# A fused two-layer PEER/MLA trunk: one placed list of stage parts, and each addition of v given to an engine by a model of both

## The reference, cut to what matters

```python
S, D, DEPTH = 512, 1024, 2            # tokens, width, layers
def peer_mixer(h, w_q, sub_keys, u, v):          # both layers
    q = (h @ w_q).reshape(B, S, 8, 2, 128)
    s = einsum('bshpc,hpnc->bshpn', q, sub_keys)
    top_s, top_i = top_k(s, 16)
    best_s, pos = top_k(top_s[..., 0, :, None] + top_s[..., 1, None, :], 16)
    idx, gate = indices at pos, softmax(best_s)            # 8 x 16 = 128 experts per token
    a = einsum('tkd,td->tk', u[idx], h)                    # u, v: 16384 x 1024
    return einsum('tk,tkd->td', gate * gelu(a), v[idx])

for i in range(2):
    h = rmsnorm(x, mix_norm[i])
    x = x + (pool_mixer(h) if i == 0 else mla_mixer(h, ...))    # mla: 8 heads, causal, after shared_kv(x)
    x = x + peer_mixer(rmsnorm(x, ffn_norm[i]), ...)
    g = sigmoid(rmsnorm(x, ple_norm[i]) @ ple_wg[i])
    x = x + g * (p[i] @ ple_wp[i])
return rmsnorm(x, final_norm)
```

## Time and profile before

| | |
|---|---|
| median of 3 runs | 2887.83 us (2886.12 to 2888.53) |
| the profiled execution | 2894.77 us, span 2893.0 us |
| busy share of the span | PE 79%, DVE 74%, POOL 44%, ACT 37% |
| moved from HBM | 1175 MB, 1074 MB of it by the gathers |
| mean rate over the span | 406 GB/s |
| mean granted TensorE clock | 0.905 |

### The profile page before, as it was taken

The page is one execution under the profiler, slowest core; times in us unless marked ns, Lnnn a source line. Parts: engine busy times, 40 slices in busy tenths (PEclk is TensorE's granted clock), DMA queues, the critical chain, the costliest instruction groups (busy, mean ns, idle before and its releaser), DMA issues.

```text
span 2893.0 us, 23323 instructions
## 1 busy us (share of the span) xinstructions
PE 2281.1 (79%) x6572; PEld 1176.2 (41%) x6572; DVE 2142.1 (74%) x4486; ACT 1072.7 (37%) x3181; POOL 1278.6 (44%) x1029
## 2 busy tenths in 40 slices
PE   6787777977879987888687999799967788766555
PEld 4444233522534543455253455346624333222112
DVE  6877768885797667757979766676696788677776
ACT  2433324333244433632324443364332244333222
POOL 2353543454443444444433344444344344555652
PEclk8999988998999998999899999899989899987777
DMA  8999999999999999999999999999999999999995
GB/s 357 416 386 419 413 420 397 409 420 420 420 383 411 420 420 420 419 420 420 395 420 394 418 410 419 420 400 398 420 392 420 419 387 415 419 420 420 420 420 234
DMA packets 164787, 1175.37 MB, mean 406 GB/s; under 512 B 18481, under 2 KB 19889, under 8 KB 23601
## 3 DMA queue, kind: packets, MB, share of 16 engines
q0 software_dynamic: 147456, 1073.81, 90.4%
q1 hardware_dynamic: 16624, 98.24, 8.3%
q10 hardware_dynamic: 576, 1.84, 0.2%
HBM read 1171.71 MB, written 2.10 MB: 406 GB/s over the span
## 4 chain that ended last, share of the span: by engine, by line
PE 35%; DMA 34%; DVE 19%; ACT 5%; issue 4%; POOL 2%; DVEq 0%; SPq 0%; ACTq 0%; POOLq 0%
DMA slot<-in_uv,idx 34%; PE acc L931 19%; DVE slot L1638 7%; DVE X L1629 2%; PE B L685 2%; PE M L603 2%; PE B L603 2%; PE M L873 2%; POOL slot L580 2%; PE M L685 1%; ACT diag L1156 1%; PE B L873 1%; ACT w L1150 1%; DVE SD L1266 1%; DVE top_u L1271 1%
## 5 line engine op out<-in xcount | busy, mean ns | idle before, releaser
L931 PE MATMUL acc<-slot,diag 128*128 128x512 f32 x2904 | 1558.1, 677 | 576.8 <-ACT diag L1156 575.3
L580 POOL DMA_INDIRECT slot<-in_uv,idx x1024 | 1278.3, 1248 | 1571.9 <-PE acc L931 1106.0
L1638 DVE CUSTOM_DVE_ANT_0 slot<-slot,HP 128x1024 f32<-128x1024 f32 x1024 | 1244.1, 1221 | 602.6 <-DMA slot<-in_uv,idx 593.1
L931 PEld LDWEIGHTS acc<-slot,diag 128*128 128x128 f32 x2904 | 575.0, 210 | 1416.9 <-ACT diag L1156 846.0
L1148 ACT ACTIVATE act_a<-a 128x1 f32<-128x1 f32 x1024 | 206.7, 202 | 1629.7 <-DVE a L1638 1628.6
L1629 DVE SCALAR_TENSOR_TENSOR X<-slot,w,X 128x1024 f32<-128x1024 f32 x297 | 380.6, 1282 | 24.0 <-ACT w L1150 23.9
L1150 ACT ACTIVATE w<-act_a,gate 128x1 f32<-128x1 f32 x1024 | 301.7, 295 | 33.2
L1156 ACT ACTIVATE diag<-cst,w 128x128 f32<-128x128 f32 x726 | 291.5, 402 | 23.8
L685 PE MATMUL B<-TT,w 128*128 128x256 f32 (+1 forms) x448 | 88.0, 351 | 0.0
L685 PE MATMUL M<-TT,w 128*128 128x256 f32 (+1 forms) x448 | 87.3, 349 | 0.0
L685 PEld LDWEIGHTS B<-TT,w 128*128 128x128 f32 x448 | 77.3, 193 | 20.6 <-issue 13.0
(11 more groups left out here) (201 smaller groups left out, 1559.9 us busy)
## 6 DMA issues: line engine op xcount, KB each, us to landing
w<-in_wq SPq DMA_DIRECT2D x28, 1024.0 KB, 9.1
slot<-in_uv,idx POOLq DMA_INDIRECT x1024, 14.3
w<-in_ple_wg SPq DMA_DIRECT2D x8, 1024.0 KB, 9.0
w<-in_w_o SPq DMA_DIRECT2D x8, 1024.0 KB, 9.2
w<-in_w_dq SPq DMA_DIRECT2D x6, 1024.0 KB, 9.5
w<-in_w_uq_nope SPq DMA_DIRECT2D x8, 768.0 KB, 8.5
w<-in_ple_wp SPq DMA_DIRECT2D x5, 1024.0 KB, 10.5
slot<-in_wq SPq DMA_DIRECT2D x4, 1024.0 KB, 15.6
```

The lines of the kernel that those rows point to most:

```text
L580: nc.gpsimd.indirect_dma_start(out=slot[s][:], out_offset=None, in_=uv[g // NC], in_offset=bass.IndirectOffsetOnAxis(ap=idx[:, g % HPB, k: ...
L931: last = nc.tensor.matmul(acc[:, half * 512:half * 512 + 512], diag[adds_on_pe(n) % DIAGS][:], slot[s][:, D + half * 512:D + half * 512 + ...
L1638: nc.vector.tensor_tensor_reduce(out=slot[s][:, 0:D], in0=slot[s][:, 0:D], in1=HP[:, g % HPB, :], scale=1.0, scalar=0.0, op0=ALU.mult, op1 ...
```

## The change

1. **One list.** `STEPS`, `BESIDE`, `PARTS`, `LATER` and the two lanes go. `PASSES[g]` is one list of (stage, part). `WORK` gives for each part its microseconds on VectorE and on PE; `weight` turns that into gathers, and `starts_of` lays the parts one after the other by their weights (those after `rank1` stretched by up to 1.4), up to gather 112. The rank stages stand in the list like the others: `asked_second` puts `rank1` behind `asks1`, and `woven` mixes the rank stages of the next chunk among the keys, queries or gates.
2. **Additions.** `adders` walks the pass with a clock for VectorE and one for PE, adds each part's work where it stands, and gives each addition of v to VectorE where PE is further behind by more than 0.3 us, else to PE. The counts per pass become 24, 23, 46, 51, 46, 55, 28 and 16 (289 in all, 298 before).
3. **Norms.** ScalarE squares all chunks of a stage first (with a `STEP` between) and takes one square root over them; before, one root for each chunk.
4. **Small steps.** More `STEP`s and part borders in `pool`, `fnorm` and `trig` on VectorE.

The pieces of weights, their order and the total of bytes are the same, as is the work except for the square roots.

```diff
-ADDS_ON_DVE = (32, 28, 32, 44, 32, 42, 26, 64)
+DVE_HEAD, DVE_TAIL = 3, 2
...
+WORK = {
+    "pool": lambda g, n: [(0, 0), (1, 0)] + [(2.6, 3.7), (2.3, 3.7)] * n + [(2.6, 0)],
...
+DVE_FREE, PE_FREE, DVE_ADD, PE_ADD, DOT = 1.4, 0.9, 1.3, 1.75, 1.3
+
+def weight(st, part):
+    dve, pe = WORK[st[0]](*st[1:])[part]
+    both = (dve / DVE_ADD + pe / PE_ADD) / (DVE_FREE / DVE_ADD + PE_FREE / PE_ADD)
+    return max(both, dve / DVE_FREE, pe / (PE_FREE + PE_ADD * DVE_FREE / DVE_ADD))
...
+def starts_of(g):
+    begin, last = (0 if g == 0 else DVE_HEAD - 1), KSEL - 16
+    weights = [weight(*p) for p in PASSES[g]]
+    soon = 1 + max([-1] + [i for i, (st, _) in enumerate(PASSES[g]) if st[:2] == ("rank1", g)])
+    rest = sum(weights[soon:])
+    scale = min(STRETCH, (last - begin - sum(weights[:soon])) / rest) if rest else 1
+    scaled = [w if i < soon else w * scale for i, w in enumerate(weights)]
+    return [int(begin + sum(scaled[:i])) for i in range(len(weights) + 1)]
...
+def adders():
...
+        unit = DOT + DVE_FREE
+        dve = pe = 0.0
+        for k in range(KSEL):
+            dve = max(dve, k * unit) + stage_work[k][0] + DOT
+            pe = max(pe, k * unit) + stage_work[k][1]
+            head = g > 0 and k < DVE_HEAD
+            tail = g == PAIRS - 1 and k >= KSEL - DVE_TAIL
+            behind_dve, behind_pe = dve - k * unit - DOT, pe - dve
+            on_dve = head or tail or behind_pe > behind_dve + 0.3
+            if on_dve:
+                dve += DVE_ADD
+            else:
+                pe = max(pe, dve + 1.1) + PE_ADD
+            found.append(on_dve)
...
-            def norm(stage, g0, src, width, i=0):
+            def norms(stage, g0, srcs, width, i=0):
...
+                for j, src in enumerate(srcs):
+                    if j:
+                        yield STEP
+                        act.wait_ge(squared, n + j)
+                    nc.scalar.activation(sq_out[:, 0:width], src, ACT.Square, accum_out=ss[:, n + j:n + j + 1]
+                                         ).then_inc(squared, 1)
+                act.wait_ge(squared, n + len(srcs))
+                nc.scalar.activation(rms[:, n:n + len(srcs)], ss[:, n:n + len(srcs)], ACT.Sqrt, bias=eps,
+                                     scale=1.0 / width).then_inc(normed, len(srcs))
```

More of the change, by code:

```diff
@@ L176, with top16s @@
         "add": [("ple_wp", [0])], "wp": [("ple_wp", [0])], "tail": [("ple_wg", [0, 1, 2, 3])]}
[L181 to L204, removed]
-}
+def top16s(n):
+    return 3.3 * n
@@ L344, in begin, with finish @@
+                spread.clear()
+    def finish():
+        while spread:
+            step()
+    def begin(st, part):
+        finish()
         stage, g0, n = st
@@ L961, in fnorm_stage @@
                 act.wait_ge(x_ready, before("x_ready", "fnorm", g0))
-                for i in range(n):
-                    norm("fnorm", g0, X[:, (g0 + i) % NC, :], D, i)
+                yield from norms("fnorm", g0, rows(g0, n), D)
                 yield
@@ L1004, in latent_stage @@
                 act.wait_ge(x_ready, before("x_ready", "latent", g0))
-                for i in range(n):
-                    norm("latent", g0, X[:, (g0 + i) % NC, :], D, i)
+                yield from norms("latent", g0, rows(g0, n), D)
                 for _ in range(4):
@@ L1009, in latent_stage @@
                 act.wait_ge(weights_used, used("w_dkv", g0, 0))
-                for i in range(n):
-                    norm("latent", g0, MB[i][:, 0:KVR], KVR, n + i)
+                yield from norms("latent", g0, [MB[i][:, 0:KVR] for i in range(n)], KVR, n)
             def keys_stage(g0, n):
@@ L1028, in dq_stage @@
                 act.wait_ge(weights_used, used("w_dq", g0, 2))
[L1029 to L1030 removed]
+                yield from norms("dq", g0, [MB[i][:, 0:QR] for i in range(n)], QR)
             def uq_stage(g0, n):
@@ L1085, in enorm_stage @@
                 act.wait_ge(x_ready, before("x_ready", "enorm", g0))
-                for i in range(n):
-                    norm("enorm", g0, X[:, (g0 + i) % NC, :], D, i)
+                yield from norms("enorm", g0, rows(g0, n), D)
                 yield
@@ L1100, in add_stage @@
                 if g0 >= NC:
-                    for i in range(n):
-                        act.wait_ge(x_ready, before("x_ready", "add", g0) + i + 1)
-                        norm("add", g0, X[:, (g0 + i) % NC, :], D, i)
+                    act.wait_ge(x_ready, before("x_ready", "add", g0) + n)
+                    yield from norms("add", g0, rows(g0, n), D)
                     yield
@@ L1112, in tail_stage @@
                 act.wait_ge(half_summed, 2)
-                norm("tail", g0, X[:, c, :], D)
+                yield from norms("tail", g0, rows(g0, 1), D)
                 act.wait_ge(hat_scaled, 1)
```

227 lines of the change are left out of this document (127 added, 100 removed).

## The result

The kernel with the change takes 2921.94 us (median of 4 runs, 2916.32 to 2923.66), before it is 2888.18 us in the same comparison: 1.0106 times as long, with an interval of 1.009 to 1.0121. That is 31 us **slower** (the two medians themselves stand 33.8 us apart), where I had forecast 25 us less and a range up to 2884 us. The profiled execution has a span of 2921.8 us. It is the slowest of its four, and the profile of the kernel before lies 6.6 us above its median, so a length read from one profile is good to some us only.

What follows compares the result with a forecast made beforehand. The prediction took the DMA roof of 420 GB/s as the bound. Its terms, -20.4 - 10.6 + 3.5 + 4 - 1.3 = -24.8 us from a median of 2887.8, gave 2863 us, forecast 2852 to 2870, range 2842 to 2884.

Steps and rivals of the forecast that it cites:

- The prediction's own sign of being wrong: Middle slices lose 45 us or more in new places, or the last pass runs under 420 GB/s with PE full.
- The bound: Whole kernel: DMA at 420 GB/s is the roof, 2798 us of the span's 2893; only the middle's 51.8 us is open.
- The rank stretches: Six stretches with rank stages lost 30.7 us; moving stages and additions leaves a third and takes back 20.4 us.
- PE's stages and the scattered losses: Pooling, attention of the last chunk and scattered places lost 10.0 + 11.2 us; half, 10.6 us, is recovered.
- The block of 25.8: Passes 2 and 4, gather 56: worst remaining VectorE block, 25.8 us of work, nearly fits 25 to 28 us of DMA.
- Norm and scaling: Ten places start norm and reciprocal at one gather; VectorE waits at least 4.1 us each; +4 us, 0 to 8.
- The fewer square roots: ScalarE saves 15 of 37 square roots of 0.29 us on an engine at 37%; effect nothing.
- The ring: Pass 0, third query of asks1: closer weight-buffer reuse makes PE stand about 5.4 us; +3.5 us overall, 0 to 7.
- The tail: End of the last pass: one late VectorE addition instead of two ahead of the last dot; -1.3 us.
- B: Rival: loss moves more than it goes, new holes from PE rows and norm waits; about 2877 us, chance 0.17.
- C: Rival: the model puts additions wrongly, so gains and new waits cancel; 2884 to 2893 us, chance 0.08.
- D: Rival: TensorE's clock stays low in the last pass, so PE bounds it; about 2902 us, chance 0.09.

Runs made afterwards that it cites:

- run 3: The change with at least 2.5 gathers for each part whose result another engine takes up next: 2914.81 us, 1.0098 times the kernel before.
- run 11: The kernel before with only the merged square root, and the STEP between the squares, added: 2894.65 us, 1.0021 times the kernel before.
- run 8: The change with passes 2 to 5 placed in the old two lanes, merged root kept: 2888.16 us, 0.9998 times the kernel before.
- run 4: The change with one square root per chunk again and no STEP between the squares: 2916.64 us, 1.0107 times the kernel before.
- run 1: The change's new placement with the old, evenly spread additions: 2953.85 us, 1.0225 times the kernel before.
- run 2: The old two-lane placement of the kernel before, with additions given out by the model: 2891.74 us, 1.0007 times the kernel before.
- the three repairs and the single root: The change with handover gaps, longer heads, half weight for rank stages of chunks 2 to 7, and one root per chunk: 2895.09 us, 1.0027 times before.
- run 5: The change with the parts of attention (heads) weighing 1.5 times as much in the list: 2909.19 us, 1.0064 times the kernel before.
- run 6: The change with the rank stages of chunks 2 to 7 at half weight in the list: 2909.75 us, 1.0071 times the kernel before.
- run 7: The change with the edits of run 3, run 5 and run 6 together, merged root kept: 2895.02 us, 1.0015 times the kernel before.

## Why the prediction was wrong

In short: the terms for VectorE's full blocks held, and the kernel still got slower, because the sum priced each engine's work in a block and put the handovers between engines, and attention's new density, at next to nothing. In lost time of the middle slices the 31.5 us (51.8 to 83.3) are: rank stages -23.4, where I had -20.4; the two places at gathers 58 to 70 +26.1, where the prediction had them nearly fit; the two at `dq` +12.8, under a term of +4 for all norms; the rest, mostly attention, +16, where I had -10.6. The prediction's own sign of being wrong, a middle that loses 45 us or more in new places, came true, and a third of that loss at the places that it named first.

*The bound: right.* The DMA roof of 420 GB/s stood in every kernel, and in each the 38 middle slices hold the difference. The kernel is as long as 2798 us plus what the DMA engines stand idle.

*The rank stretches, -20.4: right.* A third of 30.7 us was to be left. In the rows after, rank stages at 1367 and 2140 us run at 419 and 420 GB/s with VectorE at 82%, where the rate was 357 and 360; what still stands beside a rank stage (470, 2343 and 2493 us) is 7.3 us.

*PE's stages and the scattered losses, -10.6: this step failed*, and it was a guess of a half with no reading behind it. There were 10.0 + 11.2 us of this sort; after, all that is not at a rank stage is 83.3 - 7.3 = 76 us, so all of this grew by 55 us. Of the 76, 26.1 and 12.8 are taken up in the next two paragraphs; what is left, 37, set against 21.2, is the term itself: +16 instead of -10.6. I wrote that "attention and pooling are spread no thinner than before" and did not ask whether they stood **denser**. They did: attention of pass 5's second chunk went from gathers 35 to 58 to gathers 29 to 48. A stretch with PE at 100% was the warning, and the experiment with longer heads gave some 12 us back.

*The block of 25.8: right place, wrong price.* I named gathers 56 to 63 of passes 2 and 4 as the worst and wrote that "they nearly fit". The stretches there (gathers 58 to 70) cost 12.5 and 13.6 us, nearly half of the new loss. The sum of VectorE's work was not the error: over 903 to 942 us VectorE is busy only 87%, PE 81%. What I had not counted is order between engines: gates, sigmoid, product, addition and norm are a chain over three engines, and each engine keeps its own queue of gelus, additions and dots behind the link that it waits for. Adding up an engine's work in a window of eight gathers can't see this.

*Norm and scaling, +4 (0 to 8): right kind, too small.* The total of these waits was to be "well over 23 us, up to 56"; it was 83.2. I had priced 4.1 us for two squares, table load and root. I did not see that the squares wait in turn for PE: at `dq`, 11.35 us of VectorE, of which 7.25 are ScalarE waiting for PE's product. The two places cost 12.8 us; they went with the gaps of run 3 (419 GB/s in pass 2). The table load was priced well: the root at 915.00 us begins 1.30 us after its load began at 913.70, as in the tail before. The Trainium skill, page "ScalarE: Activation LUTs", section "What ACT_TABLE_LOAD costs", adds a drain of about 1.38 us; this trace has no room for it between the two.

*The fewer square roots, nothing: wrong.* I costed the saved instructions and not the wait that a shared one adds: 6 to 7 us in the kernels of runs 11 and 8, with the `STEP` between the squares; on the change's own placement (run 4) no difference is shown.

*The ring, PE standing 5.4 us: right; the price of +3.5: not shown.* The third query of pass 0 stood 5.28 us for `wq`. From 112 to 119 us the rate is 420 GB/s all the same, and pass 0 as a whole is 2.1 us shorter, so the wait was hidden or outweighed; the distance was not tried alone.

*The tail, -1.3.* The last dot begins 27.9 us before the end of the span, as before (27.7). Pass 7 is 0.4 us shorter. Too small to be told.

*Rivals.* B ("the loss moves more than it goes") has the mechanism that happened, but I let 13 us of new loss arise where it was some 55. C is refuted by runs 1 and 2: the model's additions are a help where the places are bad and neutral elsewhere. D did not happen. From 2600 to 2736 us the clock was 0.97, PE did 213 records in 105.52 us, 1.98 us per addition of four, and the rate was 420; so at that clock PE did not fall behind. The Trainium skill, page "TensorE: Matmul & The Clock Gate", section "What's actually happening", has activity release the throttle; the trace agrees, with 0.97 at PE 78% busy where it was 0.74 at 62%.

What stays open: on the change's own placement the three repairs and the single root still leave 0.27% to before, in passes 2 to 4, and in pass 5 against its usual 353 us. I have not taken this apart further. That order between engines is the cause rests on the timelines, on run 3 (waits and one hole gone, the total hardly changed) and on runs 5 to 7 (room gives 26 of 31 us back); no run moved the handovers apart with all else held.

## What to carry to other kernels

A placement by each engine's total work prices the wrong thing where a stage is a chain over several engines: give the receiving part its distance in time, since every engine queues unrelated work behind the one that waits. When a planner relieves one resource, look at which parts paid with their room: a list that must be compressed takes it from all alike, and here the dense and the chained stages broke first. And test a planner's two outputs apart, here places and additions, since a good half can hide a bad one: 34 us of gain stood in front of 65 us of loss.

## What was not expected of the hardware

A short stop of PE can cost more than itself. The query at 112.99 us, after 5.28 us of standing, took 5.85 us where the one ahead took 3.74. The gates at 880.91 us after 2.17 us took 5.40 instead of 3.60, and the two additions at 907.70 us after 6.93 us took 6.14, for 3.60 in the earlier trace rows. The granted clock of these windows:

```profile
880.00:889.00 9.00, 8.09 (x15) 3.55 (x16) 5.08 (x8) 1.78 (x3) 1.87 (x2) 0.81 1.01 413
905.00:914.00 9.00, 6.14 (x8) 2.20 (x8) 6.26 (x8) 4.39 (x11) 3.55 (x3) 0.62 0.81 268
112.00:119.00 7.00, 6.01 (x33) 5.91 (x34) 6.92 (x15) 2.31 (x9) 2.11 (x2) 0.62 1.02 420
```

At 0.62 most of the window is at the lower level of 1.2 GHz. So in these three places the engine that made the others wait comes back slower just when they have caught up with it, by 2 us or so. A ring wait of 5.28 us is one of 7.4. The slow restart is frequent but no rule: of the 32 places of this trace where PE had stood 2 to 8 us and then did eight matmul records of 512 columns of one line, 22 took over 4.5 us instead of 3.60; after 4 us or more it was all ten.
